# Longer runs of the value products in ten head pairs of a two-layer hybrid attention kernel, and latent queries from five products

## What is computed

```python
def mla_q(zcq, g, w_uq, tabs):
    q = (rms_norm(zcq, g) @ w_uq).reshape(B, L, MLA_HEADS, MLA_NOPE + MLA_ROPE)
...
    s = jnp.einsum('bqkgd,blkd->bkgql', qblk, k).astype(jnp.float32) * scale
    p = jax.nn.softmax(s, axis=-1).astype(v.dtype)
    return jnp.einsum('bkgql,blkd->bqkgd', p, v)
```

## Time and profile before

| | |
|---|---|
| median of 3 runs | 954.07 us (953.35 to 954.11) |
| the profiled execution | 948.69 us, its span 946.6 us |
| granted TensorE clock | 0.995 |
| busy: TensorE, weight loads, VectorE, ScalarE, GpSimd | 96%, 68%, 59%, 45%, 54% |
| attention of layer 0 | about 247 to 465 us |
| attention of layer 1 | about 705 to 893 us |

### The profile page before, as it was taken

One profiled execution on the slowest core, in us unless ns is written; L12 is line 12 of the kernel. 1 busy time (PEld: TensorE's weight loads), 2 busy tenths in 40 slices (PEclk: granted clock), 3 DMA queues, 4 the chain that ended last, 5 costly groups with the idle time before them and its releaser, 6 DMA issues.

```text
span 946.6 us, 13414 instructions
## 1 busy us (share of the span) xinstructions
PE 906.8 (96%) x4647; PEld 643.3 (68%) x4647; DVE 560.1 (59%) x903; ACT 429.5 (45%) x879; POOL 509.3 (54%) x433
## 2 busy tenths in 40 slices
PE   4999999999999999999999899999998999999996
PEld 3787767889745565665678789888984445555684
DVE  6569043513678679963318838567247758983347
ACT  5332121413566466655334853235335646655432
POOL 3246233324677645565547438455439876666572
PEclk9999999999999999999999999999999999999998
DMA  9968561314524200010343212323343221020252
GB/s 319 293 231 273 210 247 50 84 34 105 132 52 101 51 18 18 18 68 1 145 171 110 103 32 76 81 76 84 80 116 77 70 49 26 18 76 1 91 177 89
DMA packets 51753, 95.83 MB, mean 101 GB/s; under 512 B 9508, under 2 KB 24720, under 8 KB 50664
## 3 DMA queue, kind: packets, MB, share of 16 engines
q1 hardware_dynamic: 51688, 94.99, 33.1%
HBM read 71.32 MB, written 4.21 MB: 80 GB/s over the span
## 4 chain that ended last, share of the span: by engine, by line
PE 80%; DVE 7%; ACT 6%; POOL 2%; issue 2%; DMA 1%; SPq 1%; POOLq 0%; ACTq 0%; DVEq 0%
PE banks L998 14%; PE banks L1000 13%; PE banks L999 13%; PE banks L1293 13%; PE banks L1315 11%; PE banks L1238 4%; ACT area_z L1852 2%; PE banks L1009 2%; PE banks L1334 2%; PE banks L1267 1%; DVE negmax L2245 1%; PE banks L1327 1%; ACT late_bias L1829 1%; DMA w_raw<-in_w_in_dram 1%; DVE area_b L2422 1%
## 5 line engine op out<-in xcount | busy, mean ns | idle before, releaser
L1961 POOL TENSOR_TENSOR w_split<-w_raw,w_split 128x512 fp32r<-128x512 f32 (+4 forms) x122 | 146.8, 1212 | 216.2 <-ACT w_split L1570 216.2
L998 PE MATMUL banks<-w_split,area_a 128*128 128x512 f32 (+3 forms) x612 | 232.2, 379 | 6.3 <-POOL w_split L1961 3.2
L1000 PE MATMUL banks<-w_split,area_a 128*128 128x512 f32 (+3 forms) x612 | 224.9, 367 | 0.0
L999 PE MATMUL banks<-w_split,area_a 128*128 128x512 f32 (+3 forms) x612 | 224.3, 367 | 0.0
L2245 DVE TENSOR_REDUCE negmax<-banks 128x1 f32<-128x768 f32 x160 | 148.0, 951 | 79.7 <-PE banks L1238 55.9
L1570 ACT ACTIVATE w_split<-w_raw 128x512 fp32r<-128x512 f32 (+4 forms) x122 | 69.0, 580 | 195.8 <-PE banks L1000 183.5
L1688 ACT ACTIVATE area_z<-banks 128x512 f32<-128x512 f32 x196 | 108.2, 599 | 77.8 <-PE banks L1293 74.6
L998 PEld LDWEIGHTS banks<-w_split,area_a 128*128 128x128 f32 x612 | 115.5, 189 | 39.0 <-issue 19.1
L1293 PE MATMUL banks<-area_a 97*128 97x512 f32 (+4 forms) x448 | 127.8, 401 | 4.2 <-ACT area_z L1688 3.1
L1000 PEld LDWEIGHTS banks<-w_split,area_a 128*128 128x128 f32 x612 | 115.4, 188 | 16.5
L999 PEld LDWEIGHTS banks<-w_split,area_a 128*128 128x128 f32 x612 | 115.7, 189 | 12.8
(11 more groups left out here) (234 smaller groups left out, 1454.1 us busy)
## 6 DMA issues: line engine op xcount, KB each, us to landing
w_raw<-in_w_in_dram SPq DMA_DIRECT2D x32, 512.0 KB, 3.6
area_g<-in_w_ada_dram SPq DMA_DIRECT2D x13, 1024.0 KB, 5.3
area_g<-in_w_ada_dram SPq DMA_DIRECT2D x16, 512.0 KB, 5.5
w_raw<-in_w_out_dram SPq DMA_DIRECT2D x16, 512.0 KB, 4.8
area_a<-parts SPq DMA_DIRECT2D x72, 96.0 KB, 2.2
area_a<-parts SPq DMA_DIRECT2D x30, 192.0 KB, 3.6
area_b<-in_x_dram SPq DMA_DIRECT2D x8, 512.0 KB, 6.7
w_raw<-in_w_in_dram SPq DMA_DIRECT2D x8, 352.0 KB, 5.3
```

The costliest lines, as they stand in the source:

```text
L998: nc.tensor.matmul(dst, a[0], b[0], start=first, stop=False)
L999: nc.tensor.matmul(dst, a[0], b[1], start=False, stop=False)
L1000: return nc.tensor.matmul(dst, a[1], b[0], start=False, stop=last)
L1961: op = nc.gpsimd.tensor_tensor(lo, raw, hi.bitcast(F32), ALU.subtract)
```

## The change

Ten pairs (p = 2, 3, 4, 7, 8 of both layers) become "wide". In a wide pair of layer 0 TensorE does scores 0, 1, 2 in a row, then the context products and the denominators of the pair before in a row, scores 3, the transposes, mix 0, 1, 2 in a row, scores 4, 5, ctx in a row, and mix 3, 4, 5. In a wide pair of layer 1 it does scores 0, then what is left of the pair before (`steps_left`: mix 3, 4, 5 after a wide pair, 4, 5 otherwise) and its denominators, scores 1, 2, 3, the transposes, mix 0, 1, 2, scores 4, 5; its mix 3, 4, 5 wait for the next pair. ScalarE's list and `RING` follow. `sum_last` moves to the pair's own end for pairs 2 and 3 too. The query weights are cut at 128 and 64 rows; the 64 rows are loaded twice, under each other, and the high and low part of the 64 compressed rows stand under each other in one block, so that two products do the second half: five in all. GpSimd's split of the second piece moves from pair 0 to pair 3. At the start GpSimd's split of the second weight slice waits for the first modulated rows.

```diff
-UQ = 96
+UQ = 128
...
-    return not 4 <= p < 7
+    return not 2 <= p < 7
+
+
+def wide(p):
+
+    return p in (2, 3, 4, 7, 8)
+
+
+def steps_left(L, p):
+
+    if L < DEPTH - 1:
+        return []
+    return [3, 4, 5] if wide(p) else [4, 5]
...
+        if now and wide(_p):
+            held = 3 if ctx else 1
+            RING += [("s", _L, _p, s, u) for s in range(held) for u in range(2)]
+            RING += [("x", _L, _p - 1)] if ctx else []
             RING += [("d", _L, _p - 1)]
+            RING += [("s", _L, _p, s, u) for s in range(held, 4) for u in range(2)]
...
+                        sp.dma_start(flat[0:rest], w_uq[L, UQ:RANK_Q, :]).then_inc(done, 16)
+                        sp.dma_start(flat[rest:2 * rest], w_uq[L, UQ:RANK_Q, :]).then_inc(done, 16)
...
-                        for j in range(2):
-                            mm = three(dst, [uq[:, i, j, h * P:(h + 1) * P] for i in range(2)],
-                                       [cmp_t[0:UQ, 2 * i + j, tokens(g)] for i in range(2)], j == 0, j == 1)
+                        w = [[uq[:, i, j, h * P:(h + 1) * P] for i in range(2)] for j in range(2)]
+                        three(dst, w[0], [cmp_t[:, 2 * i, tokens(g)] for i in range(2)], True, False)
+                        both = cmp_t[:, 1, tokens(g)]
+                        nc.tensor.matmul(dst, w[1][0], both, start=False, stop=False)
+                        mm = nc.tensor.matmul(dst, w[1][1], both, start=False, stop=True)
...
+                    if wide(p):
+                        wide_pair(L, p)
+                        continue
...
-                    else:
-                        mix(L, p - 1, 4)
-                        mix(L, p - 1, 5)
+                    for step in steps_left(L, p - 1):
+                        mix(L, p - 1, step)
...
+            def wide_pair(L, p):
+
+                context = L < DEPTH - 1
+                scores(L, p, 0)
+                max_tile(L, p + 1, 6)
+                if context:
+                    scores(L, p, 1)
+                    max_tile(L, p + 1, 7)
+                    scores(L, p, 2)
+                    max_tile(L, p + 1, 8)
+                    max_rows(L, p + 1, 3)
+                    mix(L, p - 1, "ctx")
+                elif wide(p - 1):
+                    max_rows(L, p + 1, 2)
+                for step in steps_left(L, p - 1):
+                    mix(L, p - 1, step)
+                denominators(L, p - 1)
+                if context:
+                    max_rows(L, p + 1, "ctx")
+                else:
+                    max_rows(L, p + 1, 3)
+                    scores(L, p, 1)
+                    max_tile(L, p + 1, 7)
+                    scores(L, p, 2)
+                scores(L, p, 3)
+                max_tile(L, p + 2, 0)
+                turn_denominators(L, p - 1)
+                turn_output(L, p - 1)
+                max_tile(L, p + 2, 1)
+                turn_max(L, p + 1)
+                if not context:
+                    max_rows(L, p + 2, 0)
+                for step in range(3):
+                    mix(L, p, step)
+                max_rows(L, p + 2, 1 - context)
+                if head_pair(p + 3):
+                    mla_head(L, 2 * p + 6)
+                scores(L, p, 4)
+                max_tile(L, p + 2, 2)
+                scores(L, p, 5)
+                max_tile(L, p + 2, 3)
+                if head_pair(p + 3):
+                    mla_head(L, 2 * p + 7)
+                if context:
+                    scores(L, p, "ctx")
+                max_tile(L, p + 2, 4)
+                if context:
+                    max_rows(L, p + 2, 1)
+                    for step in range(3, 6):
+                        mix(L, p, step)
+                    max_rows(L, p + 2, 2)
+                max_tile(L, p + 2, 5)
...
+                    if wide(p) and not context:
+                        copy_latents(L, p - 1)
+                        copy_denominators(L, p - 1)
                     exponent(L, p, 1)
...
                     for s in chunks[0][:NW]:
+                        if s[3] == 1:
+                            pool.wait_ge(h_ready, N_H[0, 0, 0])
                         split_w(s)
...
-                    if p == 0:
-                        for j in range(2):
-                            split_w(("uq", L, j, 0))
+                    if p in (0, 3):
+                        split_w(("uq", L, int(p > 0), 0))
```

More of the change, by code:

```diff
@@ L291 @@
 for _n, _p in enumerate(PIECES):
-    _landed[_n % NRAW] += 16 * (len(CHUNKS[_p[2]]) if _p[0] == "in" else 1)
+    _landed[_n % NRAW] += 16 * (len(CHUNKS[_p[2]]) if _p[0] == "in" else 2 if _p[0] == "uq" and _p[2] else 1)
     RAW_VALUE[_p] = _landed[_n % NRAW]
@@ L371 @@
         now, last = _p < NPAIR, _p > 0
[L372 to L378, removed]
-            RING += [("d", _L, _p - 1)]
-        if now:
-            RING += [("s", _L, _p, 3, u) for u in range(2)]
+        if now and wide(_p):
+            held = 3 if ctx else 1
+            RING += [("s", _L, _p, s, u) for s in range(held) for u in range(2)]
+            RING += [("x", _L, _p - 1)] if ctx else []
+            RING += [("d", _L, _p - 1)]
+            RING += [("s", _L, _p, s, u) for s in range(held, 4) for u in range(2)]
+        else:
+            if now:
+                RING += [("s", _L, _p, s, u) for s in range(2) for u in range(2)]
+            if last and ctx:
+                RING += [("x", _L, _p - 1)]
+            if now:
+                RING += [("s", _L, _p, 2, u) for u in range(2)]
+            if last:
+                RING += [("d", _L, _p - 1)]
+            if now:
+                RING += [("s", _L, _p, 3, u) for u in range(2)]
         if last:
@@ L722, in load_piece @@
                 elif kind == "uq":
-                    sp.dma_start(slot[0:UQ].rearrange("p a n -> p (a n)")[:, 0:576],
-                                 w_uq[L, a * UQ:(a + 1) * UQ, :]).then_inc(done, 16)
+                    flat = slot.rearrange("p a n -> p (a n)")[:, 0:576]
+                    if a == 0:
+                        sp.dma_start(flat, w_uq[L, 0:UQ, :]).then_inc(done, 16)
+                    else:
+                        rest = RANK_Q - UQ
+                        sp.dma_start(flat[0:rest], w_uq[L, UQ:RANK_Q, :]).then_inc(done, 16)
+                        sp.dma_start(flat[rest:2 * rest], w_uq[L, UQ:RANK_Q, :]).then_inc(done, 16)
                 elif kind == "ukv":
@@ L965, in w_views @@
                 return [(src[:, z], hi[:, z], lo[:, z]) for z in range(2)]
-            src = flat[0:UQ, 0:576].rearrange("p (h n) -> p h n", h=6)
+            src = flat[:, 0:576].rearrange("p (h n) -> p h n", h=6)
             hi, lo = (uq[:, i, a, :].rearrange("p (h n) -> p h n", h=6) for i in range(2))
@@ L1141, in turn_compressed @@
                 _, L, j, g = use
-                a, b = [(0, 96), (96, 192), (192, 320), (256, 352)][j]
+                a, b = [(0, UQ), (UQ, RANK_Q), (192, 320), (256, 352)][j]
                 freed(pe, use)
@@ L1791, in attend @@
                         mla_high(L, 2 * p + 4)
+                    if wide(p) and not context:
+                        copy_latents(L, p - 1)
+                        copy_denominators(L, p - 1)
                     exponent(L, p, 1)
-                    if context:
+                    if not wide(p) and context:
                         copy_context(L, p - 1)
-                    else:
+                    elif not wide(p):
                         copy_latents(L, p - 1)
@@ L1799, in attend @@
                     exponent(L, p, 2)
-                    copy_denominators(L, p - 1)
+                    if wide(p) and context:
+                        copy_context(L, p - 1)
+                    if context or not wide(p):
+                        copy_denominators(L, p - 1)
                     exponent(L, p, 3)
@@ L2223, in compressed_lo @@
                     dve.wait_ge(hi_ready, N_HI[use])
-                    r0, r1, hi, lo = [(0, 96, 0, 2), (0, 96, 1, 3), (0, 128, 4, 5), (64, 96, 6, 7)][j]
-                    nc.vector.tensor_tensor(cmp_t[r0:r1, lo, tokens(g)], bank(use)[r0:r1, 0:len(GROUPS[g]) * P],
+                    r0, r1, hi, lo = [(0, 128, 0, 2), (0, 64, 1, 1), (0, 128, 4, 5), (64, 96, 6, 7)][j]
+                    at = 64 if j == 1 else r0
+                    nc.vector.tensor_tensor(cmp_t[at:at + r1 - r0, lo, tokens(g)], bank(use)[r0:r1, 0:len(GROUPS[g]) * P],
                                             cmp_t[r0:r1, hi, tokens(g)].bitcast(F32), ALU.subtract).then_inc(free_dve, 1)
```

5 lines of the change are left out of this document (3 added, 2 removed).

## The result

Median 961.12 us (957.7 to 963.44, 8 runs) against 953.54 (8 runs of the kernel before); ratio 1.0079, 95% interval 1.006 to 1.0098. Slower by 7.6 us, where 2.0 faster was forecast; the time lies above the range of 945.5 to 955.8. The profiled execution took 961.07 us, its span 959.1.

What follows compares the result with a forecast made beforehand. TensorE was taken as the bound, with the chain of waits on it for 80% of the span at clock 0.995. Gains of 10.5 plus 0.2, less 8.7 of new waits, gave 2.0 us less: 952.1 us, range 945.5 to 955.8.

Steps and rivals of the forecast that it cites:

- step (g): Diff pairs 5 and 6: tiles wait for VectorE behind the first latent head; 1.0 of the queries' 3.5 us gain unfelt.
- Step (a): Layer 0, gqa pairs: scores 2 wait for ScalarE's exponential, 0.44 us in each of three pairs, 1.3 together.
- Step (b): Layer 0, pair 2: maximum rows wait for VectorE 1.5 us instead of 0.4, so 1.1 lost.
- step (c): Layer 1, pair 2: denominators are reached before VectorE's last sums end, a wait of 1.2 us.
- Step (e): Layer 1, pair 4: two mix steps of cover taken away, TensorE waits 1.3 us more before pair 5's tiles.
- Step (f): Layer 1, pairs 7 and 8: waits for an exponential, maximum tiles and sums, together 1.2 us, an estimate.
- Step (d): Layer 1, pair 3: sums with the moved split and a gate multiplication end 1.6 us late for pair 4's denominators.
- At the start: Holding GpSimd's second weight split back lets VectorE's first cast, and TensorE's first product, come earlier: 0.4 us gained.
- I take nothing: Layer 1, pair 2: VectorE 1.8 us late beside GpSimd's sums, TensorE waiting up to 1.5; priced at nothing.
- The first (gain holds): Rival: VectorE and GpSimd keep up, (b), (d), (e), (f) vanish, 7 us saved, 947; chance 0.27.
- The second: Rival: GpSimd becomes the bound in layer 1's gqa pairs, slower, 957.5 us at 0.45 lost per sum; chance 0.15.
- The third: Rival: joining narrow runs on TensorE saves nothing, 5.4 us missing, 3.4 slower, 957.5; chance 0.03.

Runs made afterwards that it cites:

- wide_l0: The changed kernel with wide pairs in layer 0 alone, none in layer 1; median 952.0 us.
- split0_wide_l1: Kernel with wide pairs in layer 1 alone, layer 1's second query piece split in pair 0 again; wait of 2.23 became 0.19, pair 3 took 16.63 for 18.67 us.
- wide_gqa: The changed kernel with only pairs 2, 3 and 4 of both layers wide, pairs 7 and 8 as before; 958.46 us.
- slow_vector_twice: Kernel without wide pairs, VectorE's second subtraction in pair 2 of layer 0 done three times in all; median 3.2 us above the kernel without wide pairs.

## Why the prediction was wrong

**Right in mechanism and size.** The run of three mix steps takes 2.72. A wide mla pair in layer 0 gains 0.50 and 0.36 for 0.54, pair 8 of layer 1 gains 0.34 for 0.5. The queries less step (g) give 0.68 + 0.36 + 0.29 in layer 0 and 0.46 + 0.25 + 0.25 in layer 1, 2.3 for 2.5. The transfer wait is worth 1.07 for 1.2. Step (a) is 0.41 for 0.44 in each of the three pairs in wide_l0's profile (an excess: what a distance of starts, 0.64, has beyond the pace of the products, 0.23). Step (b) has a wait of 1.51 for 1.5, step (c) one of 1.14 for 1.2. Step (e) has a wait of 1.36 at 800.51 where 0.33 stood before, so 1.0 for 1.3. Step (f): pairs 7 and 8 of layer 1 together are 0.3 longer, 0.2 by the forecast with their gains.

**Mis-sized.** Step (d) is 2.23 for 1.6. The cause was the one named, as split0_wide_l1 shows. Step "At the start" is 0 for 0.4. The gains of layer 1 add up to 2.6, where the forecast wrote 2.7.

**The step that failed first: "I take nothing".** In the rule against the change the forecast named a loss in pair 2 of layer 1 (VectorE 1.8 late, TensorE waiting up to 1.5) and put it at nothing, and it looked nowhere else for it. In the changed kernel these are VectorE's, first in pair 5 of layer 0, then in pair 2 of layer 1:

```profile
353.40 1.86 DVE L2350 TENSOR_TENSOR area_a<-area_b,area_a 96x768 fp32r<-96x768 f32 x1
355.19 2.02 DVE L2352 TENSOR_TENSOR area_a<-area_b,area_a 64x768 fp32r<-64x768 f32 x1
...
755.10 1.26 DVE L2409 SCALAR_TENSOR_TENSOR o_v<-o_v,lam 128x256 f32<-128x256 f32 x1
756.28 1.77 DVE L2359 TENSOR_TENSOR parts<-area_b,parts 128x512 fp32r<-128x512 f32 x1
757.97 0.94 DVE L2361 TENSOR_TENSOR parts<-area_b,parts 128x768 fp32r<-128x768 f32 x1
```

and these the same instructions in the kernel before:

```profile
347.83 0.96 DVE L2262 TENSOR_TENSOR area_a<-area_b,area_a 96x768 fp32r<-96x768 f32 x1 [1.10 <-ACT area_a L1570]
348.70 2.04 DVE L2264 TENSOR_TENSOR area_a<-area_b,area_a 64x768 fp32r<-64x768 f32 x1
...
746.56 0.48 DVE L2321 SCALAR_TENSOR_TENSOR o_v<-o_v,lam 128x256 f32<-128x256 f32 x1
746.95 0.69 DVE L2271 TENSOR_TENSOR parts<-area_b,parts 128x512 fp32r<-128x512 f32 x1
```

0.96 became 1.86, 0.48 and 0.69 became 1.26 and 1.77; the third of layer 1 stayed at 0.94 for 0.95. GpSimd's sums of layer 1 ran beside the first two. Those beside the third began 0.11 after it, and there it was GpSimd's two that took longer, 3.21 for some 2.5:

```profile
752.33 5.16 POOL L2103 TENSOR_TENSOR w_raw<-w_raw,area_z 128x512 f32<-128x512 f32 x4
758.08 3.21 POOL L2103 TENSOR_TENSOR w_raw<-w_raw,area_z 128x512 f32<-128x512 f32 x2 [0.58 <-ACT area_z L1768]
```

These are the waits that the sum lacked. At the end of pair 2 of layer 1 VectorE's first two are 1.86 longer and TensorE waits 1.06. In pair 5 of layer 0 TensorE waits 1.47. There GpSimd's sums begin 2.20 behind TensorE's context products in both kernels. The changed one, then the one before:

```profile
350.96 1.08 PE L1335 MATMUL banks<-area_z,vals 128*64 128x256 f32 x8
353.16 3.23 POOL L2103 TENSOR_TENSOR area_b<-late_bias,area_z 128x512 f32<-128x512 f32 x2 [10.69 <-ACT area_z L1768]
...
346.22 1.08 PE L1309 MATMUL banks<-area_z,vals 128*64 128x256 f32 x8
348.42 3.46 POOL L2017 TENSOR_TENSOR area_b<-late_bias,area_z 128x512 f32<-128x512 f32 x2 [11.64 <-ACT area_z L1688]
```

But VectorE's subtraction begins 2.44 behind those products (353.40) where it began 1.61 behind them (347.83), so it now lies within the sums. It starts 0.8 later and takes 0.9 longer, and by this 1.7 the tile is read later. By the rule of the Trainium skill that the forecast weighed (page "SBUF — State Buffer", section "Who interferes with whom") a VectorE instruction with two SBUF inputs contends with a GpSimd instruction that reads SBUF, and the trace agrees with it at these places too. No run moved GpSimd's sums away to test this; it rests on these rows. With 0.6 more in step (d) and 0.4 in pair 6 of layer 0 (scores that wait for ScalarE) the waits are 3.9 above the sum (by excesses, 1.7 and 1.2 for the first two): 2.1 forecast for the wide pairs, 6.0 by these, and 946.2 - 940.4 = 5.8 in "rest". Both are low. By the table the wide order adds 3.0 in layer 0 (wide_l0, no fall in that layer's attention) and 6.1 in layer 1, of which 1.6 lie behind the fall in pair 4 (21.71 without one in wide_gqa): 7.4, so 5.3 above the sum. A wait of 0.34 for ScalarE in pair 4 of layer 0 (wide_l0) is one that the list above lacks.

**The step that failed with it: a wait costed at its length.** Steps (b), (d) and (e) count the idle time of TensorE and nothing else, and the first paragraph took a clock of 0.995 as given for both kernels. The wide pairs' waits of 1.4 to 1.5 had the clock fall behind them in the profile at three places; 4.8 us of the result against before, and 12.5 - 5.8 = 6.7 against the kernel without wide pairs (5.2 and 6.4 in its two series), are in the clock at its full price, 3.3 and 4.6 at 0.68. slow_vector_twice shows the mechanism alone: 2.0 of waiting cost 5.0 in its profile and 3.2 in the median.

From -2.0 forecast to +7.6: 3.9 of waits, 0.4 at the start, 4.8 of clock, 9.1 of 9.6. With the waits by the table and the clock at 0.68 it is 5.3, 0.4 and 3.3, 9.0 of 9.6. The sum comes out either way, and the share of the clock is known only as a third to a half.

**The rivals.** The first (gain holds) fell. The second named the right place and, in part, the right reason: GpSimd was late by 2.23 once, but it has idle time in pair 2 and the loss came from VectorE's instructions that waited for it. The third fell: joining runs saved what it was priced at.

**Open.** The clock does not fall in every execution at one place: wide_l0's profile had the wait of pair 2 and no fall there, the changed kernel's and that of wide_gqa had one. Nor is it settled how much the longer runs add, or how VectorE's two slow places would look with GpSimd's sums elsewhere.

## What to carry to other kernels

Saving changes of shape on TensorE is real but small, 0.3 to 0.5 us a pair here, and it is lost at once where another engine has less slack than that: move work only where the profile shows slack on the engines that feed the next step, here pairs 7 and 8 of layer 0. Price a new wait of TensorE above its length, for the clock may be at half behind it: here 2.0 us more of waiting cost 5.0 in one profile and 3.2 on average. And take the parts of a change apart before judging it: without the wide pairs, the same change makes the kernel 4 to 5 us faster (0.9944 and 0.9968).

## What the runs showed of the hardware that was not expected

A single wait of 2.30 us, in the middle of attention, was followed by 6.8 us at 0.50 of the clock, with no gap in TensorE's work during them; one of 1.30 by none. Over all profiles 15 of 22 waits of 1.3 us and more in attention had a low stretch behind them, and 14 of 164 shorter ones of 0.6 us and more. A low stretch of 3.4 us made its pairs 1.0 to 1.6 us longer, not the full 1.7. The kernel before has some 7.7 of its 950 us as "low", start and end included, and its clock varies from 0.990 to 0.994 between its 12 executions: a part of the spread of its times. And a VectorE subtraction of two SBUF operands took 1.77 to 2.03 us instead of 0.69 to 0.96 when GpSimd's sums ran beside it.
